# Set-up of a two-block transformer kernel: x by row tiles first, parameter rows on ScalarE, memory's preparation inside the first projection

## The reference

```python
for l in range(DEPTH):
    h = rmsnorm(x, norm_mix_pre[l])
    a_in, b_x, b_b, b_c, q, k, v, gate_in = split_cols(h @ w_in[l], IN_SPLITS)
    ...
    q = apply_partial_rope(q, cos, sin)
    k = apply_partial_rope(k, cos, sin)
    br_c = dilated_attention(q, k, v) @ w_branch_c[l]
    ...
    mem_n = rmsnorm(mem, norm_memkv[l])
    x = x + rmsnorm(memory_cross_attention(rmsnorm(x, norm_mem_pre[l]), mem_n, ...), norm_mem_post[l])
    ...
```

## Time and profile before

| | |
|---|---|
| median of 3 runs | 4036.34 us (4035.73, 4036.34, 4041.52) |
| profiled execution, its own time | 4040.55 us |
| its span | 4038.7 us |
| mean granted clock of PE | 0.971 of full |
| busy PE / PEld | 3787.4 us (94%) / 3175.3 us (79%) |
| busy DVE / ACT / POOL | 2074.4 (51%) / 1276.4 (32%) / 1207.5 (30%) |
| DMA | 316.71 MB read and written, mean 78 GB/s |

### The profile page before, as it was taken

One profiled execution on the slowest core, in us unless ns is written; L12 is line 12 of the kernel. 1 busy time (PEld: TensorE's weight loads), 2 busy tenths in 40 slices (PEclk: granted clock), 3 DMA queues, 4 the chain that ended last, 5 costly groups with the idle time before them and its releaser, 6 DMA issues. The chain is left out here.

```text
span 4038.7 us, 48945 instructions
## 1 busy us (share of the span) xinstructions
PE 3787.4 (94%) x19370; PEld 3175.3 (79%) x19370; DVE 2074.4 (51%) x3443; ACT 1276.4 (32%) x2121; POOL 1207.5 (30%) x548
## 2 busy tenths in 40 slices
PE   6999988999999998899989998899999889999998
PEld 4777866888777786688867777799999778867886
DVE  4446745665654674465556665623333566633113
ACT  3233234222333323422234443311111345543222
POOL 1234432444322443244431111122222210024442
PEclk9999999999999999999999997999999989999999
DMA  3124422333222342133321001233332100112332
GB/s 92 53 71 115 133 81 62 105 105 110 82 58 70 110 135 84 58 111 108 110 77 37 27 27 37 68 94 110 94 112 89 56 18 16 28 47 84 94 94 73
DMA packets 544401, 316.71 MB, mean 78 GB/s; under 512 B 35828, under 2 KB 517167, under 8 KB 544175
## 3 DMA queue, kind: packets, MB, share of 16 engines
q1 hardware_dynamic: 526495, 278.97, 23.8%
q10 hardware_dynamic: 17680, 34.61, 2.7%
HBM read 311.44 MB, written 2.10 MB: 78 GB/s over the span
## 5 line engine op out<-in xcount | busy, mean ns | idle before, releaser
L450 POOL TENSOR_TENSOR wlo<-wraw,whi 128x1024 fp32r<-128x1024 f32 (+6 forms) x544 | 1207.3, 2224 | 2796.3 <-ACT whi L443 2795.9
L466 PE MATMUL acc<-hh,whi 128*128 128x512 f32 (+2 forms) x2744 | 1063.8, 388 | 33.9 <-DVE hl L624 25.3
L467 PE MATMUL acc<-hl,whi 128*128 128x512 f32 (+2 forms) x2744 | 1034.2, 377 | 0.0
L468 PE MATMUL acc<-hh,wlo 128*128 128x512 f32 (+2 forms) x2744 | 1034.1, 377 | 0.0
L443 ACT ACTIVATE whi<-wraw 128x1024 fp32r<-128x1024 f32 (+6 forms) x544 | 523.5, 964 | 645.6 <-DMA wraw<-in_w_up 182.4
L466 PEld LDWEIGHTS acc<-hh,whi 128*128 128x128 f32 x2744 | 521.8, 190 | 150.3 <-issue 30.8
L467 PEld LDWEIGHTS acc<-hl,whi 128*128 128x128 f32 x2744 | 521.8, 190 | 90.8 <-issue 11.8
L468 PEld LDWEIGHTS acc<-hh,wlo 128*128 128x128 f32 x2744 | 520.5, 190 | 83.7
L1526 DVE TENSOR_TENSOR t<-acc,sq 128x768 f32<-128x768 f32 (+1 forms) x44 | 36.3, 825 | 449.3 <-PE acc L468 449.3
L466 PE MATMUL ob<-hh,whi 128*128 128x512 f32 (+3 forms) x576 | 213.2, 370 | 7.2 <-DVEq L816 6.9
L466 PE MATMUL acc<-act1h,whi 128*128 128x512 f32 x528 | 209.4, 397 | 1.4 <-DVE act1l L1534 1.4
(11 more groups left out here) (391 smaller groups left out, 6221.3 us busy)
## 6 DMA issues: line engine op xcount, KB each, us to landing
wraw<-in_ffn_w SPq DMA_DIRECT2D x120, 512.0 KB, 3.7
wraw<-in_w_in SPq DMA_DIRECT2D x102, 512.0 KB, 3.8
wraw<-in_w_up SPq DMA_DIRECT2D x88, 512.0 KB, 3.7
ada_w<-in_ada_w ACTq DMA_DIRECT2D x64, 512.0 KB, 4.2
ada_w<-in_ada_w SPq DMA_DIRECT2D x32, 512.0 KB, 4.1
wraw<-in_w_down SPq DMA_DIRECT2D x32, 512.0 KB, 4.0
wraw<-in_w_out SPq DMA_DIRECT2D x16, 512.0 KB, 3.9
wraw<-in_w_mkv SPq DMA_DIRECT2D x16, 512.0 KB, 3.8
```

The source lines that it names most:

```text
L450: e.tensor_tensor(wlo[0:rows, s, a:b, 0:w], wraw[0:rows, s, a:b, 0:w], whi[0:rows, s, a:b, 0:w].bitcast(F32), ALU.subtract).then_inc(lo_re ...
L466: e.matmul(o, wh, xh, start=first, stop=False)
L467: e.matmul(o, wh, xl, start=False, stop=False)
L468: return e.matmul(o, wl, xh, start=False, stop=last)
```

## The change

What it does, in four parts.

1. **x first, by row tiles.** SP's list becomes ident, rows 0 to 127, 128 to 255 and 256 to 383 of x as three DMAs with a semaphore each, ones, the first slab, the fourth row tile of x, the further slabs. PE turns a row tile as soon as it is in: eight transposes, four to each half of `acc[r % 2]`; DVE copies the lower half (four feature tiles), ACT the upper half, 128 x 512 each.
2. **Parameter rows on ACT.** ACT issues positions, inv1, the 17 rows, edge and memory (21 DMAs) before anything else. The six parameter groups are transposed side by side into the bank `ob[0]`, between x's third and fourth tile, and copied by DVE.
3. **Angles and tables.** DVE makes the angles first of all; ACT does Sin between copies of x, then the head of slab 0, Silu last, and loads the table set with Ln and Exp before the boundary. The head of slab 1 moves into the boundary, at k = 4.
4. **Memory inside the flow.** PE's transposes of memory are hooks at tick 2 and 4, its sums at tick 7; ACT's copies are hooks at tick 3 and 5, the eight squares at tick 5 (written over `xin`), the root at tick 8. DVE waits for the root only after the flow.

The diff, cut to its core:

```diff
         def act_boundary(e, c, g, half=None):
             for k in range(KT):
+                if half and k == KT // 2:
+                    half()
                 e.wait_ge(x_ready, c.next(x_ready))
...
@@ SP
-            for n, name in enumerate(NORMS):
-                rows(0, 16 * n, A[name].rearrange("l (k p) -> (l k) p", p=P))
...
-            sp.dma_start(xin[:, :, :], A["x"][0].rearrange("(r p) d -> p r d", p=P)).then_inc(loaded, 16)
+            sp.dma_start(ident[:], A["ident"]).then_inc(ident_in, 16)
+            for r in range(3):
+                x_rows(r)
+            sp.dma_start(ones[:], A["ones"]).then_inc(loaded, 16)
...
                             load(e, c, [(0, P, rows_of(w_in, l, 0, KT, base + g * 256 + j * P))])
+                            if len(slabs) == 1:
+                                x_rows(3)
@@ PE
+            take(pe, c, acc_free)
+            pe.wait_ge(ident_in, 16)
+            for r in range(4):
+                pe.wait_ge(x_in[r], 16)
+                if r >= 2:
+                    pe.wait_ge(x_low, r - 1)
+                    pe.wait_ge(x_high, r - 1)
                 for k in range(KT):
+                    tr = pe.transpose(acc[r % 2][:, k // 4, k % 4 * P:k % 4 * P + P], xin[:, r, k * P:k * P + P], ident[:, :])
+                    if k % 4 == 3:
+                        tr.then_inc(x_turned, 1)
+                if r == 2:
+                    pe.wait_ge(loaded, 16 * N_LOADS)
+                    for t, n in enumerate(PAR_ROWS):
...
+            pe.wait_ge(set_done, len(PAR_ROWS))
+            def mem_rows(i):
...
+            def mem_sums():
+                pe.wait_ge(pt_free, c.next(pt_free))
+                for k in range(KT):
+                    pe.wait_ge(mem_sq, k + 1)
+                    pe.matmul(pt[:, 0, 0:CTX], ones[:, :], xin[:, k // 4, k % 4 * CTX:k % 4 * CTX + CTX], start=k == 0,
+                              stop=k == KT - 1).then_inc(mem_used, 1)
+            with_mem = {2: lambda: mem_rows(0), 4: lambda: mem_rows(1), 7: mem_sums}
@@ ACT
+            act.dma_start(angi[:, :], A["positions"][0].partition_broadcast(P)).then_inc(angles_in, 16)
+            act.dma_start(inv1[:], A["inv1"]).then_inc(angles_in, 16)
...
+            act.dma_start(edge[:], A["edge"]).then_inc(loaded, 16)
+            act.dma_start(min_[:, :, :], A["mem"][0].rearrange("(r p) d -> p r d", p=P)).then_inc(mem_in, 16)
+            for r in range(2):
+                x_upper(r)
+            act.wait_ge(angle_ready, 1)
+            act.activation(rope_s[:, :], red[:, :], ACT.Sin).then_inc(act_step, 1)
...
+            x_upper(2)
+            head(act, c)
+            x_upper(3)
+            act.wait_ge(set_done, len(PAR_ROWS))
             act.activation(scT[:, :, 0], par[:, 1, 82:90], ACT.Silu).then_inc(act_step, 1)
             act.activation(scT[:, :, 1], par[:, 1, 90:98], ACT.Silu).then_inc(act_step, 1)
...
+            act.preload_act_table_set("natural_log_exp_and_others")
+            act.wait_ge(x_high, 4)
+            act.wait_ge(x_low, 4)
+            act.sem_inc(x_ready, KT)
...
+            with_mem = {3: lambda: mem_copies(0), 5: mem_squares, 8: mem_rooted}
@@ DVE
+            dve.wait_ge(angles_in, 32)
...
+            for r in range(4):
+                dve.wait_ge(x_turned, 2 * r + 1)
+                dve.tensor_copy(xres[:, 0:4, r * P:r * P + P], acc[r % 2][:, 0, :].rearrange("p (k n) -> p k n", k=4)).then_inc(x_low, 1)
+                if r == 2:
+                    dve.wait_ge(par_turned, 1)
...
                 dve_flow(e, c, [], tiles_1(0), one_each(tiles_1(0)), wide=True)
+                if l == 0:
+                    e.wait_ge(rstd_ready, c.next(rstd_ready))
```

More of the change, by code:

```diff
@@ L1573, in _, with x_rows @@
             c = Counts()
-            def rows(t, r0, ap):
-                sp.dma_start(prow[r0:r0 + ap.shape[0], t, 0:ap.shape[1]], ap).then_inc(loaded, 16)
-            for n, name in enumerate(NORMS):
-                rows(0, 16 * n, A[name].rearrange("l (k p) -> (l k) p", p=P))
[L1580 to L1593, removed]
-            sp.dma_start(xin[:, :, :], A["x"][0].rearrange("(r p) d -> p r d", p=P)).then_inc(loaded, 16)
+            def x_rows(r):
+                sp.dma_start(xin[:, r, :], A["x"][0, r * P:r * P + P, :]).then_inc(x_in[r], 16)
+            sp.dma_start(ident[:], A["ident"]).then_inc(ident_in, 16)
+            for r in range(3):
+                x_rows(r)
+            sp.dma_start(ones[:], A["ones"]).then_inc(loaded, 16)
             def layer(e, l):
@@ L1947, in _ @@
                 pe.sem_inc(s, 2)
-            def turn_tokens(e, src, n):
-                take(e, c, acc_free)
-                for k in range(KT):
[L1953 to L1959, removed]
@@ L1962, in _ @@
[L1962 to L1973, removed]
@@ L1974, in _ @@
[L1974 to L1979, removed]
+            take(pe, c, acc_free)
[5 more added lines that the diff above has]
+                    pe.wait_ge(x_high, r - 1)
+                for k in range(KT):
+                    tr = pe.transpose(acc[r % 2][:, k // 4, k % 4 * P:k % 4 * P + P], xin[:, r, k * P:k * P + P], ident[:, :])
[4 more added lines that the diff above has]
+                    for t, n in enumerate(PAR_ROWS):
+                        w = PG if t == 5 else P
+                        tr = pe.transpose(ob[0][0:w, sum(PAR_ROWS[:t]):sum(PAR_ROWS[:t]) + n], prow[0:n, t, 0:w], ident[0:n, 0:n])
+                    tr.then_inc(par_turned, 1)
@@ L1980, in _ @@
             pe.wait_ge(x_ready, KT)
             give(pe, acc_free)
-            pe_stats(pe, c, CTX)
+            pe.wait_ge(set_done, len(PAR_ROWS))
+            def mem_rows(i):
+                if i == 0:
+                    pe.wait_ge(mem_in, 16)
+                for b in range(2):
+                    if i:
+                        pe.wait_ge(mem_out, b + 1)
+                    for j in range(4):
+                        k = 4 * i + 2 * b + j // 2
+                        tr = pe.transpose(ob[b][:, j * P:j * P + P], min_[:, j % 2, k * P:k * P + P], ident[:, :])
+                    tr.then_inc(mem_turned, 1)
@@ L2105, in _, with mem_copies, mem_squares, mem_rooted @@
             act.sem_inc(cond_ready, 1)
[L2107 to L2119, removed]
+            act.preload_act_table_set("natural_log_exp_and_others")
+            act.wait_ge(x_high, 4)
+            act.wait_ge(x_low, 4)
+            act.sem_inc(x_ready, KT)
+            def mem_copies(i):
+                for b in range(2):
+                    k = 4 * i + 2 * b
+                    act.wait_ge(mem_turned, 2 * i + b + 1)
+                    act.activation(xres[:, k:k + 2, SEQ:TC], ob[b][:, :].rearrange("p (k n) -> p k n", k=2), ACT.Copy)\
+                       .then_inc(mem_out, 1)
+            def mem_squares():
+                mem_copies(1)
+                for k in range(KT):
+                    if k % 2 == 0:
+                        act.wait_ge(mem_out, k // 2 + 1)
+                    act.activation(xin[:, k // 4, k % 4 * CTX:k % 4 * CTX + CTX], xres[:, k, SEQ:TC], ACT.Square).then_inc(mem_sq, 1)
+            def mem_rooted():
+                act.wait_ge(mem_used, KT)
+                act_rstd(act, c, CTX, to=rstd[:, SEQ:TC])
+            with_mem = {3: lambda: mem_copies(0), 5: mem_squares, 8: mem_rooted}
             def layer(e, l):
                 e.wait_ge(gains_ready, c.next(gains_ready))
-                act_boundary(e, c, gain(0))
-                act_flow(e, c, [], tiles_1(0), one_each(tiles_1(0)), wide=True)
+                act_boundary(e, c, gain(0), None if l else lambda: head(e, c))
+                act_flow(e, c, [], tiles_1(0), one_each(tiles_1(0)), wide=True, hooks={} if l else with_mem)
                 e.activation(ysum[:, 0:SEQ], rstd[:, 0:SEQ], ACT.Square).then_inc(rx2_ready, 1)
@@ L2217, in _ @@
                 c.start(s, 2)
[L2219 to L2229, removed]
-            dve.wait_ge(loaded, 16 * N_LOADS)
             def step(ins):
@@ L2235, in step @@
                 dve.wait_ge(dve_step, c.next(dve_step))
+            step(dve.memset(small[:, 63:64], EPS))
+            dve.wait_ge(angles_in, 32)
             step(dve.tensor_copy(ang[:, :], angi[:, :]))
@@ L2271, in layer @@
                 if l == 0:
-                    e.wait_ge(rstd_ready, c.next(rstd_ready))
                     dve_boundary(e, c, gain(0))
+                    e.wait_ge(cond_ready, 1)
+                    e.wait_ge(tables_ready, 1)
                 else:
```

54 lines of the change are left out of this document (40 added, 14 removed).

## The result

The changed kernel took **4013.47 us** (median; 4012.65 to 4015.48), the kernel before 4038.64 in the four runs beside it; ratio 0.9945, interval 0.9932 to 0.9958 (the two medians alone divide to 0.9938). Both profiled executions side by side: the span fell from 4038.7 to 4010.8, by 27.9, where the prediction had 30.75.

The account below looks back on a forecast made before the run. TensorE, busy 94% of the span, was taken to bound the kernel: hh starting 33.85 us earlier, less a flow 3.1 us longer, gives 30.75 us, so 4005.6 us on the median 4036.34; range 3999 to 4014.

Parts of the forecast that it names:

- The start, 19.7: End of the set-up: hh, the first projection's split of x, starts at 19.7 us instead of 53.55, gaining 33.85.
- does one table load of 1.28 before or behind them: Set-up, ScalarE: one 1.28 us table load around its 21 DMA issues, so its first copy starts at 11.2 us.
- lands at most 2.9 us later, the price of 288 KB: Set-up: the last of 19 loads, issued by 10.8 us, lands by 13.7, releasing the parameter transposes.
- x's tiles land at about 4.5, 5.8 and 7.0 us: Set-up: landing times of x's first three row tiles, the first one issued by 1.6 us.
- six hand-offs of 0.1: Set-up: some six hand-offs between engines, 0.1 us each, counted in the start of hh at 19.7.
- The boundary's split, 0: Boundary, k = 4: ScalarE's added 1.0 us weight split fits behind TensorE's work, costing 0, or 1.0 if uncovered.
- POOL's waits, -1.9: Flow: TensorE's four waits for POOL, 1.9 us in all, go once the table load between Ln and Exp is removed.
- Transposes 1.6, sums 3.4: Flow, TensorE: memory's 16 transposes add 1.6 us and its eight sums 3.4 us.
- The flow given back: Flow rival, 7%: ScalarE's 6.2 us of memory work delay splits, POOL, then TensorE, one for one; 4011.8 us.
- Held issues: Set-up rival, 12%: SyncE's queued DMAs hold ScalarE's queue too, hh starts 7 to 10 us later; say 4015 us.
- The low clock in the boundary: Boundary rival, 20%: TensorE's last transposes end 3 to 4 us before the first sum, so the clock is low.
- the 1.7 of the range: Boundary: 1.7 us for a full clock there, counted in the lower end of the range, 3999.

Follow-up runs that it names:

- e1: Changed kernel with ScalarE loading one table set for Copy, Sin and Silu ahead of its first copy; 4005.0 us, ratio 0.9922.
- e2: Changed kernel with SyncE holding the second and third weight slabs until all 19 constant loads have landed; 4009.3 us, ratio 0.9927.
- e5: Changed kernel with its fourth part undone, memory's transposes, sums and root ahead of the boundary again; 4009.84 us, ratio 0.9932.
- e11: Changed kernel with 32 idle transposes added in the set-up, 12 behind x's second tile, 20 behind its fourth; 4007.9 us, ratio 0.9929.
- e7: Kernel before the change, with only the preload of the Ln and Exp table set added; 4030.8 us, ratio 0.9989.
- e9: Changed kernel unedited, run again on another chip; 4007.21 us, ratio 0.9933 to the kernel before.
- e10: Changed kernel with four edits: one set-up table set, slabs held, memory's sums one tile later, second weight split ahead of the boundary; 3999.05 us, ratio 0.991.
- e4: Changed kernel with memory's eight sums one tile later, at tick 8 instead of 7; 4006.8 us, ratio 0.9927.
- e12: e10 with the idle transposes of e11 added as a fifth edit; 4004.27 us, ratio 0.9915.
- e6: Changed kernel with the second weight split ahead of x's fourth copy instead of inside the boundary; 4007.9 us, ratio 0.9933.
- e8: Changed kernel with the 17 parameter rows and edge issued by SyncE again, behind all four x tiles; 4013.4 us, ratio 0.994.
- e13: e12 without the edit of e6, so the second weight split stays inside the boundary; 4001.01 us, ratio 0.9918.

## Why the prediction was right or wrong

The median, 4013.47, is 7.9 above the forecast, and the ratio on the 4036.34 of the forecast gives 4014.1, just outside the range (3999 to 4014). On the other chip the same kernel lies at 0.9933 x 4036.34 = 4009.3. By its steps, in the profiled executions:

- **The start, 19.7: wrong by 2.92.** Right: the order, which engine waits for what, tile 2 at 13.6 (though through DVE). Failed: *"does one table load of 1.28 before or behind them"*, and only one more behind tile 3. The kernel before needed one load for Silu and Sin; with Copy and Sin coming first, ACT loads for Copy (11.11), for Sin (13.51) and again for Silu (19.62), 1.28 each, and the last stands between tile 3 and hh (e1: 1.26). Failed too: *"lands at most 2.9 us later, the price of 288 KB"*, so at 13.7. The last of these loads takes 15.89 - 10.24 = 5.7 us from issue, with x and slabs on the same engines, where I used the 2.9 of a mask that moved alone; e2 gets 0.9 back, and what made the rest late is not shown. And *"x's tiles land at about 4.5, 5.8 and 7.0 us"*: the first at 7.08, 5.9 from issue, where 2.8 and 3.8 were medians over the whole run. Positions and inv1 were as late (7.22), and the angles ended at 12.9 instead of 9.7. The two failures add up: 2.19 + 1.28 is 3.47; from the landing to hh the rest took 5.45 us, where the forecast had 6.0 with its six hand-offs of 0.1, which gives the 2.92. That 0.1 was an estimate which no run shows; from the end of tile 3 (18.97) to ACT's copy (19.00) the trace has 0.03.
- **The boundary's split, 0: 0.31.** PE waits for it at full clock in e5 and e11 as well.
- **POOL's waits, -1.9: -1.26.** The mechanism held (e7). I had taken the idle times of four weight loads (0.54, 0.49, 0.43, 0.49) as TensorE's loss; where the other 0.6 of their sum went is not shown.
- **Transposes 1.6, sums 3.4.** Their loads last 1.03 + 1.02 and 3.33. c went from 51.24 to 56.42, 5.2 where 5.0 was forecast: right.
- **The flow given back:** false. c is the sum of its parts to 0.2 us, no tile waits for ACT.
- **Held issues:** true in kind only. SP's last slab issues took 3.26 for two and x's fourth tile 2.80; ACT's 21 issues ended at 11.09, 1.1 us later than 21 of 0.44. ACT's DMAs are a queue of their own in the DMA view of the changed kernel (up to 30 us 1359 packets, 1.58 MB, beside SP's 5168), but the two are not independent: with the slabs held (e2) the rows landed at 14.99 instead of 15.89. The forecast has no term for slabs against the rows, where it cost 0.9.
- **The low clock in the boundary, the rival at 20%:** the 1.7 of the range was an estimate from the 0.72 granted over 54 to 60 us, 0.28 of 6.0 us; measured, the boundary at full clock is 1.64 shorter (b 13.50 before, 11.86 in e7). The rival's price, up to 1.7 more than before, no run shows; it was -0.07 in the profiled run, +0.9 in e9. The rival was real, though not shown to cost more than before on the whole, and I had put its cost in the wrong place too: the low clock also costs 1.1 ahead of hh. That the clock can rise under transposes, as the forecast read from the earlier trace rows, e11 shows again: with nothing on PE but transposes since 7 us, its loads fell from 0.2 to 0.11 us and stayed there to the last of them; e2 shows the same fall for tile 2 (0.86 for eight) without added transposes.
- **What lies behind the scores, 0 by the forecast:** 3919.1 against 3918.0 in the profiled executions, but that was luck. The forecast allowed 3 us between executions in its range; d alone has a spread of 16.

In sum: -33.85 became -30.93; +3.1 became +4.2 (b 0.24, c 3.92); d -1.1; together -27.9 in the spans. With start, boundary and flow as measured the forecast would have been 4005.6 + 2.92 + 0.24 + 0.82 = 4009.6.

**What stays open.** Why d differs. It is not an edit: none touches it. In the eight traces with a low clock at the end of the flow (as in the window above) d is 3914.2 to 3921.2; in the six without it 3905.0 to 3916.5. The low time behind the scores is 202 us in the two lowest (e7, e10) and 221 to 238 in eleven others, and a microsecond of low clock, at 0.50 granted, costs at most half of one; e4, at 207, is third lowest in both. So the clock may carry much of it, but among the eleven the order of low time is not that of d (e1 has most, with 3914.2; e12 has 232, with 3916.5), and the records miss low stretches (below). What places the low stretches in later layers is not shown, and no experiment could hold a and c fixed and move only them.

## What to carry to other kernels

When the order of a set-up changes, list ACT's functions in their new order and count the table loads between them: one preload of a set that holds them all gave 1.26 us at the first hh, and one preload of Ln and Exp gave 6.4 at the scores in the old order (one load in place of four, and with them the low clock of the boundary). Price the landing of small late DMAs from a stretch in which the queues are as full as they will be, not from a lonely transfer (5.7 us here against 2.9). And before a few microseconds at the start are counted as a gain at the end, run the unedited kernel again on the chip of the experiment: here 3.6 and 5.1 us at the scores could not be told in the time, and of the 8.2 us by which e10 leads e9 only 2.5 stand at the scores.

## What the hardware showed that was not expected

- An idle time need not bring the clock down: behind 2.86 us in e11 the first statistics ran at full clock, behind 4.45 in e12, with the same added transposes, at half clock (1.10 and 2.05 us).
- The granted clock in the records can miss the first low stretch: in e6, e8, e9 and e10 the first statistics lasted 2.04 or 2.05 us, as at half clock, while the windows give 1.00 over them. The duration of a weight load of known form (0.19 or 0.34 us for 128 x 128, at 27.64 and at 24.99 in the changed kernel, granted 1.00 from 28 on and 0.50) tells the level.
- Positions, 256 KB spread over all partitions, landed 4.9 us after issue and inv1, 0.5 KB behind it in the queue, after 6.0: the tiny one came in behind the large one ahead of it, and the angles waited for it.
- A wait that two edits each leave harmless can appear between them: holding slabs (e2) and splitting the second slab early (e6) made ACT stand 1.35 us in e10 and 2.09 in e12, the two that have both, and not in e2, e6 or e13.
